# A four-unit first opening: a fourth weight unit taken inside, four scale rows on TensorE, and the start's loads reordered

## What is computed

```python
def sandwich(x, y_fn, g_pre, g_post, shift, scale, gate, resid_w):
    h = rmsnorm(x, g_pre) * (1.0 + scale) + shift
    return x + resid_w * gate * rmsnorm(y_fn(h), g_post)

for l in range(DEPTH):
    mod = (jax.nn.silu(c) @ w_ada[l] + b_ada[l]).reshape(B, 9, 1, D_MODEL)
    x = sandwich(x, lambda h: swiglu(h, ffn1_w_in[l], ffn1_w_out[l]),
                 g[0], g[1], mod[:, 0], mod[:, 1], mod[:, 2], 0.5)
    ...
```

## Time and profile before

| | us |
|---|---|
| median of 3 runs (2697.83 to 2698.90) | 2698.54 |
| the profiled execution | 2698.14 |
| its span, first to last instruction | 2696.40 |
| PE busy in the span | 2665.8 (99%) |
| DVE busy | 1496.3 (55%) |
| ACT busy | 1127.7 (42%) |
| POOL busy | 257.7 (10%) |

### The profile page before, as it was taken

One profiled execution on the slowest core, in us unless ns is written; L12 is line 12 of the kernel. 1 busy time (PEld: TensorE's weight loads), 2 busy tenths in 40 slices (PEclk: granted clock), 3 DMA queues, 4 the chain that ended last, 5 costly groups with the idle time before them and its releaser, 6 DMA issues.

```text
span 2696.4 us, 37221 instructions
## 1 busy us (share of the span) xinstructions
PE 2665.8 (99%) x13120; PEld 2154.4 (80%) x13120; DVE 1496.3 (55%) x2530; ACT 1127.7 (42%) x2048; POOL 257.7 (10%) x333
## 2 busy tenths in 40 slices
PE   8999999999999999999999999999999999999999
PEld 6888887677777888888888888877777778888887
DVE  7665445667746656533366563565787375553323
ACT  4332245666555353222252222547655443532222
POOL 0111000112100001110011110002221000011100
PEclk9999999999999999999999999999999999999999
DMA  8555523112222416433245545221112224242332
GB/s 299 212 188 193 156 96 95 63 56 64 72 94 71 117 55 248 172 100 103 93 168 191 195 155 164 97 85 57 63 65 77 87 76 114 101 162 94 100 102 70
DMA packets 94795, 321.82 MB, mean 119 GB/s; under 512 B 16769, under 2 KB 17153, under 8 KB 93378
## 3 DMA queue, kind: packets, MB, share of 16 engines
q1 hardware_dynamic: 94658, 320.07, 35.9%
HBM read 316.72 MB, written 2.13 MB: 118 GB/s over the span
## 4 chain that ended last, share of the span: by engine, by line
PE 88%; DVE 6%; ACT 2%; issue 2%; DVEq 1%; DMA 0%; POOL 0%; SPq 0%; ACTq 0%; POOLq 0%
PE bank L513 20%; PE bank L515 20%; PE bank L514 19%; PE bank L522 7%; PE bank L520 7%; PE bank L521 7%; PE bank L2009 2%; PE bank L1988 2%; DVE w_low L497 1%; PE bank L1979 1%; DVEq L1160 1%; PE bank L1966 1%; DVE scores_sb L1347 1%; PE bank L1711 1%; ACT w_high L490 1%
## 5 line engine op out<-in xcount | busy, mean ns | idle before, releaser
L513 PE MATMUL bank<-h_high,w_high 128*128 128x512 f32 x2248 | 896.0, 399 | 2.1 <-DVE h_low L1551 1.5
L515 PE MATMUL bank<-h_high,w_low 128*128 128x512 f32 x2248 | 877.0, 390 | 0.0
L514 PE MATMUL bank<-h_low,w_high 128*128 128x512 f32 x2248 | 875.6, 390 | 0.0
L497 DVE TENSOR_TENSOR w_low<-w_raw,w_high 128x1024 fp32r<-128x1024 f32 x423 | 547.2, 1294 | 562.3 <-ACT w_high L490 559.2
L490 ACT ACTIVATE w_high<-w_raw 128x1024 fp32r<-128x1024 f32 x423 | 443.9, 1051 | 358.6 <-PE bank L522 312.7
L513 PEld LDWEIGHTS bank<-h_high,w_high 128*128 128x128 f32 x2248 | 422.7, 188 | 99.5 <-issue 12.8
L515 PEld LDWEIGHTS bank<-h_high,w_low 128*128 128x128 f32 x2248 | 421.9, 188 | 90.2
L514 PEld LDWEIGHTS bank<-h_low,w_high 128*128 128x128 f32 x2248 | 422.8, 188 | 83.8 <-issue 1.9
L520 PE MATMUL bank<-w_high,ffn_high 128*128 128x512 f32 x704 | 274.4, 390 | 0.0
L522 PE MATMUL bank<-w_low,ffn_high 128*128 128x512 f32 x704 | 274.0, 389 | 0.0
L521 PE MATMUL bank<-w_high,ffn_low 128*128 128x512 f32 x704 | 273.9, 389 | 0.0
(11 more groups left out here) (237 smaller groups left out, 2966.8 us busy)
## 6 DMA issues: line engine op xcount, KB each, us to landing
w_raw<-stream SPq DMA_DIRECT2D x438, 512.0 KB, 3.6
ada_raw<-ada SPq DMA_DIRECT2D x128, 512.0 KB, 3.6
ada_start<-ada SPq DMA_DIRECT2D x8, 1024.0 KB, 18.1
post_gain<-post_gain_row SPq DMA_DIRECT2D x6, 512.0 KB, 5.6
mixer_consts<-mixc SPq DMA_DIRECT2D x2, 1152.0 KB, 5.3
x<-x_in SPq DMA_DIRECT2D x4, 512.0 KB, 6.5
silu_c<-silu_row SPq DMA_DIRECT2D x4, 512.0 KB, 4.2
out<-x SPq DMA_DIRECT2D x8, 256.0 KB, 2.0
```

The costliest lines, as they stand in the source:

```text
L497: eng.tensor_tensor(low[:, :], raw[:, slot], high[:, :].bitcast(F32), ALU.subtract).then_inc(lo_ready[slot].sem, 1)
L513: eng.matmul(o, a, rhs_h, start=first, stop=False)
L514: eng.matmul(o, a, rhs_l, start=False, stop=False)
L515: return eng.matmul(o, b, rhs_h, start=False, stop=last)
```

## The change

- SP: the identity is loaded first, with a semaphore of its own; then blocks 0 and 1 of x, then `c_row`, the parameters and c's column, then blocks 2 and 3. Units 0 and 1 come behind group 0, unit 2 behind group 1, unit 3 behind group 3. ACT makes the two tanh between the squares of blocks 1 and 2.
- Scale rows 0 to 3 are made on PE (`PE_ROWS = 4`). On PE, row 1 stands behind the products of units 0 and 1 with h row 0, rows 2 and 3 stand at the head of k = 1 and k = 2. The host packs the scale rows 2 and 3 accordingly.
- Unit 2 runs one row behind units 0 and 1. Unit 3 runs inside the opening, by the table `FOURTH_AT`, and PE's `turn(0)` no longer takes it.
- ACT splits unit 1 after row 0, unit 2 after row 1, unit 3 after row 2. DVE splits units 0 and 1 in row 0, unit 2 in row 1 (behind that row's `vec_scale`), unit 3 in row 3.
- The fills are six, then two, of x's block 0 instead of eight, three and five single ones of `c_row`; they begin when block 0 of x is there.

```diff
-PE_ROWS = 2
+PE_ROWS = 4
+FOURTH_AT = {3: [0], 4: [1, 2], 5: [3, 4], 6: [5], 7: [6]}
...
         def _(sp):
-            sp.dma_start(c_row[:, :], cvec.partition_broadcast(P)).then_inc(consts_in.sem, 16)
-            sp.dma_start(parv[:, 0:3 * KD], par0).then_inc(consts_in.sem, 16)
-            sp.dma_start(skt[:, 0:KD], ccol).then_inc(consts_in.sem, 16)
-            sp.dma_start(ident[:, :], consts[:, 0:P]).then_inc(consts_in.sem, 16)
+            sp.dma_start(ident[:, :], consts[:, 0:P]).then_inc(ident_in.sem, 16)
             for tb in range(TB):
                 sp.dma_start(x[:, tb], x_in[:, tb]).then_inc(x_loaded[tb].sem, 16)
+                if tb == 1:
+                    sp.dma_start(c_row[:, :], cvec.partition_broadcast(P)).then_inc(consts_in.sem, 16)
+                    sp.dma_start(parv[:, 0:3 * KD], par0).then_inc(consts_in.sem, 16)
+                    sp.dma_start(skt[:, 0:KD], ccol).then_inc(consts_in.sem, 16)
 
             for g in range(KD):
                 sp.dma_start(ada_start[:, 2 * g:2 * g + 2], ada0[:, 2 * g:2 * g + 2]).then_inc(ada_start_in[g].sem, 16)
-                if g == 0:
-                    for u in range(LEAD):
-                        sp.dma_start(raw[:, u], stream[u]).then_inc(raw_full[u].sem, 16)
-            sp.dma_start(raw[:, LEAD], stream[LEAD]).then_inc(raw_full[LEAD].sem, 16)
+                for u in ((0, 1), (2,), (), (LEAD,))[g] if g < 4 else ():
+                    sp.dma_start(raw[:, u], stream[u]).then_inc(raw_full[u].sem, 16)
...
-            s.wait_ge(consts_in.sem, 16 * 4)
-            s.activation(skt[:, KD:2 * KD], skt[:, 0:KD], ACT.Tanh, scale=0.5).then_inc(c_tanh.sem, 1)
-            s.activation(silu_start[:, :], c_row[:, :], ACT.Tanh, scale=0.5).then_inc(c_tanh.sem, 1)
-
             for tb in range(TB):
+                if tb == 2:
+                    s.wait_ge(consts_in.sem, 16 * 3)
+                    s.activation(skt[:, KD:2 * KD], skt[:, 0:KD], ACT.Tanh, scale=0.5).then_inc(c_tanh.sem, 1)
+                    s.activation(silu_start[:, :], c_row[:, :], ACT.Tanh, scale=0.5).then_inc(c_tanh.sem, 1)
                 s.wait_ge(x_loaded[tb].sem, 16)
...
                 s.activation(hH[:, j], tu[:, j % 2], ACT.Copy).then_inc(start_hh.sem, 1)
-                if j == 0:
-                    for u in range(1, LEAD):
-                        split_high(s, 0, u)
-            split_high(s, 0, LEAD)
+                if j < LEAD:
+                    split_high(s, 0, j + 1)
...
                 if j == 0:
                     split_low(v, 0, 0)
                     start_low(0)
-                    for u in range(1, LEAD):
-                        split_low(v, 0, u)
-                elif j >= 2:
-                    start_low(j - 1)
+                    split_low(v, 0, 1)
+                else:
+                    if j == 1:
+                        split_low(v, 0, 2)
+                    if j > 1:
+                        start_low(j - 1)
+                    if j == LEAD:
+                        split_low(v, 0, LEAD)
             start_low(KD - 1)
-            split_low(v, 0, LEAD)
...
-                    pe.matmul(bank[b][:, :], ident[:, :], c_row[:, 0:T], start=True, stop=True)
+                    pe.matmul(bank[0][:, :], ident[:, :], x[:, 0, 0:T], start=True, stop=True)
...
-            fill(8)
+
+            def unit_product(u, k):
+
+                if k == 0:
+                    unit_ready(pe, 0, u)
+                mm = product(pe, bank[u][:, :], weights(0, u), k * P, slice(0, P), hH[:, k], hL[:, k], k == 0, k == KD - 1)
+                if k == KD - 1:
+                    mm.then_inc(unit_done[u].sem, 1)
+            pe.wait_ge(x_loaded[0].sem, 16)
+            fill(6)
             pe.wait_ge(silu_col_ready.sem, 1)
             scale_row(0)
             pe.wait_ge(start_xn[0].sem, 2)
             pe.wait_ge(start_xn[1].sem, 2)
             for j in range(4):
                 x_tile(j)
-            fill(3)
-            slots = None
+            fill(2)
             for k in range(KD):
-                if k + 1 < PE_ROWS:
-                    scale_row(k + 1)
                 if 4 <= k + 3 < KD:
                     x_tile(k + 3)
+                if 1 <= k < PE_ROWS - 1:
+                    scale_row(k + 1)
                 pe.wait_ge(start_h.sem, k + 1)
+                unit_product(0, k)
+                unit_product(1, k)
                 if k == 0:
-                    slots = [unit_ready(pe, 0, u) for u in range(LEAD)]
-                for j, slot in enumerate(slots):
-                    mm = product(pe, bank[j][:, :], weights(0, j), k * P, slice(0, P), hH[:, k], hL[:, k], k == 0, k == KD - 1)
-                    if k == KD - 1:
-                        mm.then_inc(unit_done[slot].sem, 1)
-                if PE_ROWS - 1 <= k < KD - 2:
-                    fill(1, 3)
+                    scale_row(1)
+                if k >= 1:
+                    unit_product(2, k - 1)
+                for k4 in FOURTH_AT.get(k, ()):
+
+                    unit_product(LEAD, k4)
+            unit_product(2, KD - 1)
+            unit_product(LEAD, KD - 1)
...
-                    turn(0, range(LEAD, 4))
+                    turn(0, range(LEAD if f or l else LEAD + 1, 4))
```

More of the change, by code:

```diff
@@ L352, in trunk_kernel @@
         consts_in = sig("consts_in", 0)
+        ident_in = sig("ident_in", 0)
         x_loaded = [sig(f"x_loaded{i}", 0) for i in range(TB)]
@@ L1529, in _ @@
             b1 = mod_sum
-            v.wait_ge(consts_in.sem, 16 * 4)
+            v.wait_ge(ident_in.sem, 16)
+            v.wait_ge(consts_in.sem, 16 * 3)
             v.tensor_scalar(b1[:, :], parv[:, KD:2 * KD], 1.0, None, ALU.add)
@@ L1738, in first_opening, with fill @@
         def first_opening(pe):
-            def fill(count, b=0):
+            def fill(count):
                 for _ in range(count):
-                    pe.matmul(bank[b][:, :], ident[:, :], c_row[:, 0:T], start=True, stop=True)
+                    pe.matmul(bank[0][:, :], ident[:, :], x[:, 0, 0:T], start=True, stop=True)
             def scale_row(j):
@@ L2017, in _ @@
                 pe.sem_inc(unit_done[slot].sem, 1)
-            pe.wait_ge(consts_in.sem, 16 * 4)
+            pe.wait_ge(ident_in.sem, 16)
             first_opening(pe)
```

## The result

The changed kernel is slower: 2707.32 us, the median of 8 runs (2706.18 to 2708.15), against 2698.60 for the kernel before in the same job (8 runs, 2697.08 to 2700.66). The ratio is 1.0032, 95% interval 1.0023 to 1.0040, so +8.7 us. The forecast was +3.8. The profiled execution took 2708.15 us, its span 2706.4, which is 10.0 more than before; what follows is the account of those 10.0. It is the longest of the eight, with a mean granted clock of 0.995 where the other seven have 0.996 or 0.997, and the profile of before has 1.000, so a little of the 10.0 belongs to these two executions and not to the medians.

A forecast was written before the change was run, and what follows sets the result against it. PE was taken to bound the kernel, so the start of unit 4 decides: 57.3 - 53.5 = +3.8 us, on the median 2698.54 + 3.8 = 2702.3 us. The range was 2697.5 to 2706.5.

The forecast's parts named there:

- a shift of the opening is kept to the end: Behind the opening: PE is busy 2665.8 of 2696.4 us, so a shift of its work shifts the result.
- second table load: ACT's start: Square as first function instead of Tanh needs none; one would cost at most 1.3 us.
- DVE stood still for ACT's split of unit 2: Opening, row 1: DVE waits 2.6 us for ACT's half, delaying row 2's reduction and h_low of row 1.
- scale row 3 behind the products of k = 1: Opening, k = 2 on PE: DVE's vec_scale of row 3 waits for it and loses 3.2 us.
- the walk: Engine-by-engine timeline of the opening, first 54 us: unit 4 starts at 57.3 instead of 53.5, +3.8 us.
- Leaving out the loop's fills: Opening's loop: the fills cost nothing to lose as work, since PE waits there anyway.
- PE's clock: Rival: PE falls to 1.2 GHz in the new gaps from k = 1; +6.0, 2704.5, or 2706.3 with scale row 3; chance 0.26.
- all behind it moves: Clock rival, k = 1: nine products at half rate add 2.2 us, shifting everything later, to +6.0.
- The range: Whole kernel: 2697.5 to 2706.5 us, taking in the forecast, the given back and most of the clock rival.
- a doubly slow clock: Part of the clock rival left outside the range; scale row 3 slow too adds 1.8, 2706.3; the first gap could add as much.
- Row 0 stays: Start of the opening: scale row 0 stays at 14.95 and h_high of row 0 at 18.84.
- The floor: Opening, rival that DVE doesn't wait: PE alone is the bound, unit 4 at 49.5, -4.0, 2694.5; chance 0.10.

The follow-up runs named there:

- e10_lit: Changed kernel with fills breaking up PE's light stretches (scale rows and tiles only) as well as its idle ones; 2703.83 us, ratio 1.0015.
- e4_no_loop_fills: Kernel before without the five fills inside its loop; 2698.95 us, ratio 1.0002.
- e5_shift4: Kernel before with five more fills behind the opening's products, a bare shift of 4.3 us; 2704.37 us, ratio 1.0018.
- e1_fills: Changed kernel with fills where PE stands still: eight at the start, four ahead of h row 1, two ahead of h row 3; 2708.47 us, ratio 1.0037.
- e9_loads_only: Kernel before with only the new order of the loads up to x, and the tanh and fills that go with it; 2700.22 us, ratio 1.0004.
- e7_fourth_only: Kernel before with only the fourth unit taken inside the opening, two fills kept; 2697.43 us, ratio 0.9995.
- e2_split_late: Changed kernel with DVE's split of unit 2 moved behind row 1's low part; 2704.43 us, ratio 1.0021.
- e3_two_rows: Changed kernel with two scale rows on PE instead of four, rows 2 and 3 reduced by DVE; 2705.23 us, ratio 1.0025.
- e6_shift8: Kernel before with nine more fills behind the opening's products, a bare shift of 7.7 us; 2708.61 us, ratio 1.0035.
- e11_lit_split_late: Changed kernel with DVE's split of unit 2 behind row 1's low part and fills breaking PE's light stretches; 2704.10 us, ratio 1.0016.
- e12_fourth_lit: Kernel before with the fourth unit inside the opening and one fill between scale row 0 and the transposes; 2698.30 us, ratio 0.9995.
- e13_lit_two_rows: Changed kernel with DVE's split of unit 2 late, two scale rows on PE, and fills in the gaps of k = 1 to 3; 2701.00 us, ratio 1.0005.

## Why the prediction was wrong

**Right, by its own steps.** PE bounds the kernel and a shift of the opening is kept to the end (8.0 us from 61 to 428). The first functions took no second table load. h_low of row 1 came at 29.95 (29.75), k = 1 at 30.68 (30.5); DVE stood still for ACT's split of unit 2 (2.51 for 2.6) and then for scale row 3 behind the products of k = 1. From there the distances are the walk's as well: row 2 to row 7 15.76 us (15.75), row 7 to unit 4 6.50 (6.45). At full clock, in e10_lit, unit 4 is within 0.2 us of the walk. Leaving out the loop's fills cost nothing in the order of before (e4_no_loop_fills).

**The step that failed: PE's clock.** It was made a rival with 0.26 on the ground that "small matmuls and 1.7 us waits didn't lower it". Two things were wrong with that. First, it rests on one profile of before, in which scale row 0 and four tiles, 32 small matmuls between the fills of the earlier trace rows, left the clock at full. That was luck of the draw: of the four later profiles with the same start, two have a fall there (16.4 to 19.9 in e4_no_loop_fills, 17.4 to 20.8 in e5_shift4). The change adds another such stretch, scale row 1, a tile and scale row 2, 36 small matmuls from 22.70 to 27.18, and then the gap. The clock fell at 26.4 within that stretch. In e1_fills the gap was filled and the clock fell all the same; in e10_lit the stretch was broken as well and it didn't. Nor is this one draw: all eight runs of the changed kernel have a mean clock of 0.997 or less, all ten of e10_lit 0.999 or more. So idle time isn't needed for a fall, and a stretch of small matmuls can do it, though not each time. The idle 3.5 us came too late to start the fall; that they made it long is likely and rests on two profiles: e1_fills was back at full for k = 1 (matmuls 0.23 apart from 31.20), the changed kernel stayed at half until 43.4, with only nine products and again a scale row in between. The Trainium skill, "TensorE: Matmul & The Clock Gate", section "Why this matters for your kernels", names idle gaps as what to avoid. The changed kernel has such a gap, 3.50 us, but its clock fell 0.8 us before the gap began, and in e1_fills it fell without one: the rule points the right way and isn't the whole of it here.

Second, the price of the rival. In the opening its total was right, partly by luck: 2.2 and 1.8 were given for the nine products and scale row 3, 4.0 together; they cost 1.83 and 1.57, and a tile at half rate that it left out 0.50, 3.9 together. What it lacked is the fall in the mixer, 1.6 in the profile, which the prediction didn't foresee at all: "all behind it moves" was taken as a plain shift at full clock. 2698.14 + 3.8 + 3.9 + 1.6 is 2707.4 of the 2708.15 measured.

**The range** ended at 2706.5 because it left out "a doubly slow clock", half of a rival that came out whole. The gap was known to be twice the longest of before, so the rival deserved more than 0.26, and its upper end needed a term for later falls.

**Row 0 stays** was right only in sum: it started 1.0 earlier in this profile (13.92 for 14.95), and lost that again by the tiles at half clock (3.60 us for 1.97). The two cancelled by luck; e9_loads_only didn't find the early start again.

**The floor** of -4.0 "if DVE doesn't wait" was not reached by any kernel, and the change without any wait wasn't tried. The best, e7_fourth_only, has 2.5 at unit 4 and 1.7 in the median, which the interval doesn't separate from no change.

## What to carry to other kernels

PE can be busy in every window of the profile and its clock fall all the same: here it fell behind stretches of small matmuls. So before small matmuls are gathered in one place, read the granted clock behind every such stretch, in more than one profile, and price the matmuls that follow at half rate. On an engine that runs its list in order, an operation that waits for another engine belongs behind whatever the bottleneck engine is waiting for: moving one split behind one low part brought the low part of h row 1 2.9 us nearer to its `vec_scale`. When a kernel bound by one engine is shifted, time a bare shift of the same size too, and compare runs of like mean clock: here that told the shift's own cost from that of falls elsewhere.

## What was not expected of the hardware

- The clock fell with PE busy, behind 24 to 36 small matmuls and tiles (26.4 in the changed kernel, 26.3 in e1_fills, 429.2 in the mixer). Most falls lasted about 3.4 us, and among dense products one cost 1.6; some were longer (6.8 us at the start of e2_split_late and of e3_two_rows, 10.2 in the latter's opening), and the one of the changed opening lasted 17.0 us (26.4 to 43.4) although 17 matmuls of products ran in it, in two groups with a tile and a slow scale row between them.
- The same 24 small matmuls of a mixer lower the clock in some kernels and not in others. In single profiles, the clock fell in the first mixer in the changed kernel, e1_fills, e2_split_late, e3_two_rows, e6_shift8, e11_lit_split_late and e12_fourth_lit, and didn't in the kernel before, e4_no_loop_fills, e5_shift4, e7_fourth_only, e9_loads_only, e10_lit and e13_lit_two_rows. In the second mixer it fell in e1_fills, e3_two_rows, e5_shift4 and e9_loads_only to e13_lit_two_rows. The size of the shift doesn't sort them (e12_fourth_lit is 1.9 us early and fell in both mixers). Whether the moment at which they run decides it, or chance from run to run, wasn't told apart, with one profile of each kernel.
- The scatter of the kernel before goes with its mean clock. Of its 94 runs in the four jobs, 23 have 1.000 and take 2696.9 to 2698.3 us, 55 have 0.999 and take 2698.6 to 2700.0, and 16 have 0.998 or less and take 2700.3 to 2702.9. That fits none, one and two or more falls of 3.4 us; where in the kernel they lie in these runs isn't shown, since only its profile at 1.000 was kept.
